# An index projection cut into blocks of 256 and 328 columns, its loads and gating transposes in another order, weight splits without one of their waits, and the first expert picks computed earlier

## The chip, the cores and the metric

One core of a Trainium2 chip runs the whole program. The metric is the device time of one execution in microseconds. The core has TensorE (PE in the profile; PEld is its loading of stationary operands), VectorE (DVE), ScalarE (ACT), GpSimd (POOL) and SyncE (SP), whose only work here is to issue DMAs. Line numbers such as L936 are those of the kernel before; behind the change they shift by one to some ten lines.

## What is computed

The program computes three transformer layers over 256 tokens of width 1024, in float32. The parts that the change touches are the input projection of the first layer, its expert layer, and the weights' preparation everywhere:

```python
q, k, v, qi, ki, wi, su, sv, ga, gb = split_columns(rms_norm(h, g) @ w_in)   # widths 1024 x3, 512, 64, 8, 1024 x4
qi, ki = rope(qi), rope(ki)                       # 8 index heads of 64, one key of 64
rel = relu(einsum('bqhd,bsd->bqhs', qi, ki)); score = einsum('bqh,bqhs->bqs', wi, rel)
sel = top_k(causal(score), 64)                    # then attention of q over the chosen keys, values
mixed = einsum('gts,bcsgd->bctgd', tril(sgu_w), layer_norm(gelu(sv))) + b_s   # gating weights sgu_w
g_sel = argmax(x @ w_group); e_in_group = (x @ w_er)[g_sel]; top2 -> experts, softmax -> gates
ys = (silu(x @ w_in[e])[:256] * ...) @ w_out[e]; out += gates * ys            # 32 experts, 2 per token
```

Behind the first layer come two more: attention and cross attention with a feed-forward of 2816, then a gated linear recurrence with cross attention and the same feed-forward.

## The kernel before

**Products in three parts.** Every weight matrix is used as a high and a low part. A linear block is up to 512 output columns wide and up to 8 row chunks (k) of 128 deep per piece. `linear` issues, for each k and each of two token tiles, three matmuls: high x high (L936), low weight x high input (L937), high weight x low input (L938); so a block of 8 k is 48 matmuls. `linear_turned` does the same with the weights stationary and 256 tokens moving (L966, L968, L969).

**The supply of weights.** SyncE loads piece n (L668) into one of two ring buffers as soon as the low parts of piece n-2 are made (`raw_free`). A piece is cut into units of two k. ScalarE copies a unit to `w_high` (L1529), which needs one of 8 unit slots to be free of the matmuls on the unit 8 before it; GpSimd then subtracts it to `w_low` (L863), and only then may TensorE use the unit. Each engine runs its program in order: where ScalarE splits pieces is written out by hand between its other jobs (`split_to`, `split_units`), and so it is on GpSimd.

**The index stage.** The blocks come in the order q0, q1, qi (512 columns: the 8 index heads), kw (72 columns: index key and head weights), k0, k1. Amid k = 4 and 5 of qi, TensorE transposes the gating weights sgu_w (L984; taken by ScalarE L1629 and VectorE L2106). Amid k0, at k = 6, it transposes the late row parameters (`later_columns`), the four pairs of rotated index heads and the index key. Between kw's load and k0's load SyncE issues 19 small loads (router weights, row parameters, gains; L679 to L713).

**The router and the experts.** After the first layer's output, VectorE works out the choice of experts (L2261 to L2305): the selection, then the gates' weights (L2293 to L2298), then each token's place in its expert's list (L2301), then the number of rounds (L2302 to L2305, `router_done`). TensorE meanwhile counts with small matmuls (L1204) and runs 34 and 14 filler matmuls (`keep_running`, L1196). Then come 8 batches of 4 experts: VectorE writes `picks` (L2317) and `gates` (L2319), TensorE gathers tokens (L1214), multiplies with the first weights (L1230), with the second (L1247) and adds back (L1256). Before the first batch TensorE waits for `router_done` and reads the number of rounds into a register. Expert weights (12 MB per batch) stream in as buffers come free.

**Norms behind a projection.** After the blocks o0, fo0 (layer one of the two later ones; `post_norm`), and o1, fo1 (`post_norm_by_rows`), ScalarE squares the result and takes a root. These projections have 12 or 22 row chunks, so two or three pieces per block. In these two functions ScalarE waits, before it splits the piece after n, until TensorE has used all of piece n-1 (`pieces_used(act, n - 1)`), beside the wait that each unit has for its own slot.

Of the kernel before, what the change touches and what calls it, by code (L numbers as in the profile page):

```python
# [120 lines left out]
def program(nc, io, upto=99, tap=None):  # L121
# [115 lines left out]
    with ctx:  # L237
# [209 lines left out]
        qi_roped = tok(buf(9, 1024, 1024))  # L447
        qi_T = feat(buf(8, 1024))
        ki_twice = tok(buf(8, 256, 1168))
# [212 lines left out]
        def _(sp):  # L662
# [36 lines left out]
            for n in range(RAW, router_piece):  # L699
                if n == RAW + 2:  # L700
# [129 lines left out]
        def _(pool):  # L830
# [37 lines left out]
            split_to(2)  # L868
# [45 lines left out]
        def _(pe):  # L914
# [85 lines left out]
            def both(x):  # L1000

                return lambda i: [(P * t, x[:, t, P * i:P * (i + 1)]) for t in range(TILES)]
# [94 lines left out]
            linear("k0", *from_x, ready=amid(6, later_columns, lambda: pe.wait_ge(roped, 2), lambda: turn("qi", 4, both(qi_roped)),  # L1097
                                             lambda: turn("ki", 1, both(ki_twice))))
# [111 lines left out]
            def expert_batch(it, nth, parity, firsts, extra=False):  # L1210
# [11 lines left out]
                pe.wait_ge(moe_x, 2 * it + 2)  # L1222
                for a in range(2):
# [245 lines left out]
        def _(act):  # L1469
# [269 lines left out]
            def post_norm_by_rows(i, name):  # L1739
# [3 lines left out]
                for j in range(2):  # L1743
                    _, used, _ = blocks[f"{name}{j}"]
                    for n, _, _ in used[1:]:
                        if j == 1 and n == used[-1][0]:
                            split_to(n)
                        else:
                            pieces_used(act, n - 1)
                            split_to(n + 1)  # L1750
# [22 lines left out]
            def post_norm(i, name, late_split=False):  # L1773

                nth = (i - 5) // 2
                for j in range(2):
                    _, used, _ = blocks[f"{name}{j}"]
                    late = late_split and j == 1
                    for n, _, _ in used[1:]:
                        pieces_used(act, n - 1)  # L1780
# [203 lines left out]
        def _(dve):  # L1984
# [121 lines left out]
            tr_take(dve, 1, "sgu_w", 4, lambda i, ps: dve.tensor_copy(sgu_wT[:, SEQ * i:SEQ * (i + 1)], ps))  # L2106
# [555 lines left out]
```

## Time and profile before

| | us |
|---|---|
| median of three runs (lowest, highest) | 1335.0 (1333.69, 1336.3) |
| the profiled execution, whole | 1331.26 |
| its span in the trace | 1329.5 |
| TensorE busy within the span | 1244.0 |
| GpSimd, ScalarE, VectorE busy | 770.9, 637.9, 463.8 |
| granted TensorE clock, mean | 0.994 |

The profiled execution was 1.76 us longer than its span, and 3.7 us shorter than the median. A granted clock of 1.00 is 2.4 GHz and 0.50 is 1.2 GHz. TensorE's busy time counts pipelined matmuls by modelled ends, so how fast it really goes is read from the distance of one start to the next.

### The profile page before, as it was taken

The page shows a single profiled execution, that of the slowest core. Times are in us where ns is not written, and L with a number is a line of the kernel's source. Part 1 is how long each engine was busy: PE and PEld are TensorE (multiplying, and loading weights), DVE is VectorE, ACT ScalarE, POOL GpSimd, SP SyncE. Part 2 cuts the span into 40 slices and gives each one's busy share as a digit, 9 for nine tenths or more (in the row PEclk, how much of TensorE's full clock was granted, in tenths as well). Part 3 has the DMA queues.
Part 4 walks back from the last instruction along what each step waited for, and adds up shares of the span by engine and source line. Part 5 has one row for each costly group of instructions (what it writes and reads, how often), then busy time and mean ns, then how long its engine had stood idle before and what let it go on. Part 6 is the DMA issues. An engine that isn't in the chain of part 4 may idle for free.

```text
span 1329.5 us, 19674 instructions
## 1 busy us (share of the span) xinstructions
PE 1244.0 (94%) x7904; PEld 1022.0 (77%) x7904; DVE 463.8 (35%) x1047; ACT 637.9 (48%) x1108; POOL 770.9 (58%) x345
## 2 busy tenths in 40 slices
PE   8999999998888887999899999999999889999998
PEld 6888877776343333888789999889997778999986
DVE  3527343433121112356513333113468272322211
ACT  6345544653111011746646555446797444644452
POOL 6868985440000000981168988888689805788884
PEclk9899999999999999999999999999999999999999
DMA  7635554298999999452035655544444503455552
GB/s 252 213 128 190 190 189 158 102 364 340 422 421 377 422 422 412 179 189 80 33 127 170 211 191 183 198 174 155 163 143 174 199 8 127 157 177 176 189 190 79
DMA packets 127041, 275.09 MB, mean 207 GB/s; under 512 B 7604, under 2 KB 53996, under 8 KB 115180
## 3 DMA queue, kind: packets, MB, share of 16 engines
q1 hardware_dynamic: 126668, 272.86, 56.2%
q8 instruction: 58, 0.95, 0.3%
q10 hardware_dynamic: 288, 1.05, 0.2%
q14 instruction: 27, 0.22, 0.1%
HBM read 272.85 MB, written 1.05 MB: 206 GB/s over the span
## 4 chain that ended last, share of the span: by engine, by line
PE 73%; DMA 8%; ACT 7%; DVE 5%; POOL 4%; issue 2%; SPq 0%; POOLq 0%; DVEq 0%; ACTq 0%
PE lin_ps L936 11%; PE lin_ps L938 11%; PE lin_ps L937 11%; PE lin_ps L966 8%; PE lin_ps L969 8%; PE lin_ps L968 8%; POOL w_low L863 4%; DMA ring<-in_w_expert_in 4%; PE sc_ps L1230 3%; ACT w_high L1529 2%; DMA work<-in_w_expert_out 2%; PE lin_ps L1247 2%; PE lin_ps L1052 2%; PE sc_ps L1021 2%; PE lin_ps L1214 1%
## 5 line engine op out<-in xcount | busy, mean ns | idle before, releaser
L863 POOL TENSOR_TENSOR w_low<-ring,w_high 128x1024 fp32r<-128x1024 f32 (+1 forms) x318 | 761.5, 2435 | 467.0 <-ACT w_high L1529 466.9
L1529 ACT ACTIVATE w_high<-ring 128x1024 fp32r<-128x1024 f32 (+1 forms) x320 | 312.5, 1042 | 136.4 <-PE lin_ps L938 78.6
L966 PE MATMUL lin_ps<-x_high,w_high 128*128 128x256 f32 x960 | 272.8, 284 | 0.0
L968 PE MATMUL lin_ps<-x_high,w_low 128*128 128x256 f32 x960 | 271.6, 283 | 0.0
L969 PE MATMUL lin_ps<-x_low,w_high 128*128 128x256 f32 x736 | 208.3, 283 | 0.0
L966 PEld LDWEIGHTS lin_ps<-x_high,w_high 128*128 128x128 f32 x960 | 184.2, 192 | 0.3 <-DVEq L2442 0.2
L968 PEld LDWEIGHTS lin_ps<-x_high,w_low 128*128 128x128 f32 x960 | 184.3, 192 | 0.1
L936 PE MATMUL lin_ps<-w_high,x_high 128*128 128x512 f32 (+1 forms) x432 | 170.2, 394 | 5.2 <-POOL w_low L863 2.6
L937 PE MATMUL lin_ps<-w_low,x_high 128*128 128x512 f32 (+1 forms) x432 | 167.7, 388 | 0.0
L938 PE MATMUL lin_ps<-w_high,x_low 128*128 128x512 f32 (+1 forms) x368 | 142.8, 388 | 0.0
L969 PEld LDWEIGHTS lin_ps<-x_low,w_high 128*128 128x128 f32 x736 | 141.2, 192 | 0.0
L936 PEld LDWEIGHTS lin_ps<-w_high,x_high 128*128 128x128 f32 x432 | 82.0, 190 | 22.6 <-DVE w_low L2074 2.8
L937 PEld LDWEIGHTS lin_ps<-w_low,x_high 128*128 128x128 f32 x432 | 82.1, 190 | 15.8
L938 PEld LDWEIGHTS lin_ps<-w_high,x_low 128*128 128x128 f32 x368 | 70.0, 190 | 14.3
L1812 ACT ACTIVATE attn<-lin_ps,cols 128x256 f32<-128x256 f32 x44 | 18.5, 471 | 115.3 <-PE lin_ps L969 115.3
L936 PE MATMUL lin_ps<-w_high,hidden_high 128*128 128x512 f32 x176 | 68.7, 390 | 0.7 <-POOL w_low L863 0.7
L1230 PE MATMUL sc_ps<-ring,work 128*32 128x512 f32 x480 | 57.3, 624 | 12.2 <-DMA ring<-in_w_expert_in 7.7
L937 PE MATMUL lin_ps<-w_low,hidden_high 128*128 128x512 f32 x176 | 68.5, 389 | 0.0
L938 PE MATMUL lin_ps<-w_high,hidden_low 128*128 128x512 f32 x176 | 68.5, 389 | 0.0
L2428 DVE SCALAR_TENSOR_TENSOR attn<-lin_ps,cols,attn 128x255 f32<-128x255 f32 x44 | 21.1, 478 | 125.4 <-ACT attn L1812 125.4
L969 PE MATMUL lin_ps<-u_low,w_high 128*128 128x256 f32 x224 | 63.4, 283 | 0.0
L1230 PEld LDWEIGHTS sc_ps<-ring,work 128*32 128x32 f32 x480 | 15.3, 114 | 49.3 <-issue 36.8
(434 smaller groups left out, 1914.3 us busy)
## 6 DMA issues: line engine op xcount, KB each, us to landing
ring<-in_w_expert_in SPq DMA_DIRECT2D x30, 2048.0 KB, 15.7
ring<-in_ffn_w_in SPq DMA_DIRECT2D x44, 1024.0 KB, 7.7
ring<-in_w_in SPq DMA_DIRECT2D x13, 2048.0 KB, 7.9
ring<-in_b_w_in SPq DMA_DIRECT2D x11, 2048.0 KB, 8.0
work<-in_w_expert_out SPq DMA_DIRECT2D x8, 2048.0 KB, 23.0
ring<-in_w_expert_out SPq DMA_DIRECT2D x8, 2048.0 KB, 22.6
ring<-in_ffn_w_out SPq DMA_DIRECT2D x8, 2048.0 KB, 7.9
ring<-in_a_w_in SPq DMA_DIRECT2D x4, 2048.0 KB, 8.1
```

The lines of the kernel that those rows point to most:

```text
L863: pool.tensor_tensor(w_low[:, slot, 0:words], raw, w_high[:, slot, 0:words].bitcast(F32), ALU.subtract).then_inc(low_made, 1)
L936: pe.matmul(out[:, t, :], high(k)[:, at], wh[:, j, :], start=(k == 0), stop=False)
L937: pe.matmul(out[:, t, :], high(k)[:, at], wl[:, j, :], start=False, stop=False)
L938: mm = pe.matmul(out[:, t, :], low(k)[:, at], wh[:, j, :], start=False, stop=(k == last_k))
L966: pe.matmul(out, wh[:, j, at], high(k), start=(k == 0 and f < 2), stop=False, skip_group_check=True)
L968: pe.matmul(out, wl[:, j, at], high(k), start=False, stop=False, skip_group_check=True)
L969: mm = pe.matmul(out, wh[:, j, at], low(k), start=False, stop=(k == last_k), skip_group_check=True)
L1021: mm = pe.matmul(sc_ps[:, g % 2, SEQ * t:SEQ * t + n], q(i, t), k(i)[:, 0:n], start=True, stop=True)
L1052: mm = pe.matmul(out[:, dim * t:dim * (t + 1)], pT[:, P * n:P * (n + 1)], v(i, c), start=(c == 0), stop=(c == chunks[-1][0]))
L1230: mm = pe.matmul(hid_ps[CAP * e:CAP * (e + 1), :], gathered[:, 4 * a + k, CAP * e:CAP * (e + 1)], extra_slot(e)[k // 2][:, k % 2, :] if ex ...
L1247: mm = pe.matmul(y_ps[CAP * e:CAP * (e + 1), n, :], act_T[:, P * f + CAP * e:P * f + CAP * (e + 1)], w, start=(f == 0), stop=(f == 1))
L1529: act.activation(w_high[:, slot, 0:words], raw, ACT.Copy).then_inc(high_made, 1)
```

## The change

The index projection's 584 columns are no longer cut into 512 + 72 but into 256 (four heads) + 328 (four heads, key, head weights). The transposes of sgu_w move from qi to kw. The 19 small loads are issued behind k0's load, not ahead of it. ScalarE and GpSimd take the gating weights later. The rotated heads lie in two buffers. In the post norms the wait for whole pieces is gone. In the first expert batch VectorE makes places and picks first, then the gates, and the round count between its two gathers; TensorE's wait for the count comes ahead of the batch's first expert matmul, and its register load after the whole batch.

```diff
-            weight_block("qi", [(w_in, starts["qi"], 512)], 512)
-            weight_block("kw", [(w_in, starts["kw"], 72)], 72)
+            weight_block("qi", [(w_in, starts["qi"], 256)], 256)
+            weight_block("kw", [(w_in, starts["qi"] + 256, 328)], 328)
...
             for n in range(RAW, router_piece):
-                if n == RAW + 2:
+                if n == RAW + 3:
                     load_router()
...
-            split_to(2)
+            split_to(blocks["k0"][1][0][0])
             tr_wait(pool, "sgu_w", 4)
...
-            linear("qi", *from_x, ready=sgu_weights)
-            linear("kw", *from_x)
+            linear("qi", *from_x)
+            linear("kw", *from_x, ready=sgu_weights)
...
+                pe.wait_ge(router_done, 1)
                 for a in range(2):
...
-            pe.wait_ge(router_done, 1)
+            expert_batch(0, 0, 0, 32)
             n_rounds = pe.value_load(rounds[0:1, 0:1], min_val=1, max_val=SEQ // CAP)
-            expert_batch(0, 0, 0, 32)
             expert_batch(1, 0, 1, None, extra=True)
...
             copy_scaled("q1", half(q_raw, 1))
+            lin_ready(act, "qi")
+            split_to(piece("qi") + 2)
             tr_take(act, 0, "sgu_w", 4, lambda i, ps: act.activation(sgu_wT[:, SEQ * i:SEQ * (i + 1)], ps, ACT.Copy))
-            for name in ("qi", "kw"):
-                lin_ready(act, name)
-                split_to(piece(name) + 2)
+            lin_ready(act, "kw")
+            split_units(sum(units[piece("kw") + 2]) - 2)
             tr_take(act, 0, "qi", 4, plain(qi_T))
+            split_to(piece("kw") + 2)
...
                     for n, _, _ in used[1:]:
-                        pieces_used(act, n - 1)
                         split_to(n if late else n + 1)
...
+                dve.tensor_tensor(pick4, place, slots_iota, ALU.is_equal).then_inc(moe_pick, 1)
+                if opening:
+                    make_gates()
+                dve.wait_ge(moe_pick, it + 1)
+                dve.tensor_tensor(gate4, pick4, weight, ALU.mult).then_inc(moe_gate, 1)
...
+                    if opening and a == 0:
+                        count_rounds()
```

On ScalarE, from the sines of the rotation to the copy of k0 (L1551/L1552), the program of before and then that of the change read as follows; L1529/L1530 is the making of high parts, `xqT` the gating weights, `work<-tr_ps` the transposed index heads:

```order
L1627 ACTIVATE attn<-sc_ps 128x192
L1551 ACTIVATE work<-lin_ps,small 128x512 x2
L1529 ACTIVATE w_high<-ring 128x144 x4
L1629 ACTIVATE xqT<-tr_ps 128x256 x2
L1529 ACTIVATE w_high<-ring 128x1024 x8
L1567 ACTIVATE work<-tr_ps 128x256 x2
L1551 ACTIVATE work<-lin_ps,small 128x512 x2
L1529 ACTIVATE w_high<-ring 128x1024 x4
```

```order
L1628 ACTIVATE attn<-sc_ps 128x192
L1552 ACTIVATE work<-lin_ps,small 128x512 x2
L1530 ACTIVATE w_high<-ring 128x656 x4
L1530 ACTIVATE w_high<-ring 128x1024 x4
L1632 ACTIVATE xqT<-tr_ps 128x256 x2
L1530 ACTIVATE w_high<-ring 128x1024 x2
L1568 ACTIVATE work<-tr_ps 128x256 x2
L1530 ACTIVATE w_high<-ring 128x1024 x2
L1552 ACTIVATE work<-lin_ps,small 128x512 x2
```

The four units of kw grow from 144 to 656 words; k0's units now stand ahead of the gating weights, and two of k1's units ahead of the transposed heads.

On GpSimd, from its first constants to the mask of the scores (L876), before and after; L870 is the mask of the gating weights:

```order
L851 MEMSET eps 128x1
L863 TENSOR_TENSOR w_low<-ring,w_high 128x1024 x10
L870 AFFINE_SELECT xqT<-xqT 128x1024
L863 TENSOR_TENSOR w_low<-ring,w_high 128x144 x4
L863 TENSOR_TENSOR w_low<-ring,w_high 128x1024 x16
L876 AFFINE_SELECT attn<-attn 128x512
```

```order
L851 MEMSET eps 128x1
L863 TENSOR_TENSOR w_low<-ring,w_high 128x1024 x6
L863 TENSOR_TENSOR w_low<-ring,w_high 128x512 x4
L863 TENSOR_TENSOR w_low<-ring,w_high 128x656 x4
L863 TENSOR_TENSOR w_low<-ring,w_high 128x1024 x4
L870 AFFINE_SELECT xqT<-xqT 128x1024
L863 TENSOR_TENSOR w_low<-ring,w_high 128x1024 x12
L876 AFFINE_SELECT attn<-attn 128x512
```

The ten full units ahead of the mask become six full, four of 512 words (qi), four of 656 (kw) and four full ones (k0).

On VectorE, in the router, before and after; L2296 to L2298 (L2300 to L2302) weight the gates, L2301 (L2291) adds the places, L2302 to L2305 (L2306 to L2309) count the rounds, L2317 (L2318) writes the picks:

```order
L2295 TENSOR_TENSOR small<-small 128x2
L2296 TENSOR_TENSOR work<-work,small 128x2x32
L2297 TENSOR_TENSOR work<-work,small 128x2x32
L2298 TENSOR_TENSOR work<-work 128x2x32
L2301 TENSOR_TENSOR work<-work,sc_ps 128x2x32
L2302 TENSOR_REDUCE small<-sc_ps 128x1
L2303 TENSOR_SCALAR work<-iota,small 128x8
L2304 TENSOR_REDUCE small<-work 128x1
L2305 CAST rounds<-small 128x1
L2309 UNCONDITIONAL_BRANCH
L2309 ISA
L2317 TENSOR_TENSOR work<-work,iota 128x256
```

```order
L2291 TENSOR_TENSOR work<-work,sc_ps 128x2x32
L2318 TENSOR_TENSOR work<-work,iota 128x256
L2297 SCALAR_TENSOR_TENSOR small<-small 128x2
L2298 RECIPROCAL small<-small 128x2
L2299 TENSOR_TENSOR small<-small 128x2
L2300 TENSOR_TENSOR work<-work,small 128x2x32
L2301 TENSOR_TENSOR work<-work,small 128x2x32
L2302 TENSOR_TENSOR work<-work 128x2x32
L2322 TENSOR_TENSOR work<-work 128x256
L2326 TENSOR_TENSOR work<-lin_ps,moe_gain 128x512
L2306 TENSOR_REDUCE small<-sc_ps 128x1
L2307 TENSOR_SCALAR work<-iota,small 128x8
```

The places and the picks now come first, and the round count behind the first gather (L2326). The first two batches are written out, and the loop starts at the third.

## Rows read from the trace of the kernel before

**Rows 1.** The page: busy time of each engine, and the shares of the ending chain

```profile
PE 1244.0 (94%) x7904; PEld 1022.0 (77%) x7904; DVE 463.8 (35%) x1047; ACT 637.9 (48%) x1108; POOL 770.9 (58%) x345
...
PE 73%; DMA 8%; ACT 7%; DVE 5%; POOL 4%; issue 2%; SPq 0%; POOLq 0%; DVEq 0%; ACTq 0%
```

**Rows 2.** Windows, from:to, length; busy PE, PEld, DVE, ACT, POOL (instructions); clock; DMA; GB/s

```profile
46.40:51.80 5.40, 5.40 (x49) 5.40 (x47) 4.86 (x12) 3.90 (x4) 3.56 (x2) 0.96 0.91 304
...
51.80:56.00 4.20, 4.16 (x11) 3.28 (x11) 3.33 (x18) 0.87 (x1) 4.20 (x3) 0.50 0.32 117
...
286.00:293.00 7.00, 4.72 (x26) 3.25 (x26) 4.51 (x10) 3.22 (x8) 0.00 (x0) 1.00 0.79 296
...
326.00:328.00 2.00, 2.00 (x24) 0.52 (x16) 0.00 (x0) 0.00 (x0) 0.00 (x0) 1.00 0.00 0
...
740.00:820.00 80.00, 80.00 (x669) 80.00 (x668) 23.99 (x56) 41.87 (x70) 67.05 (x30) 1.00 0.60 197
```

**Rows 3.** Timeline of TensorE, index stage: start us, us, engine line

```profile
34.54 0.39 PE L936 MATMUL lin_ps<-w_high,x_high 128*128 128x512 f32 x1
...
34.76 0.39 PE L937 MATMUL lin_ps<-w_low,x_high 128*128 128x512 f32 x1
...
46.36 0.20 PE L936 MATMUL lin_ps<-w_high,x_high 128*128 128x72 f32 x1
...
52.16 0.80 PE L936 MATMUL lin_ps<-w_high,x_high 128*128 128x512 f32 x1
...
63.28 0.66 PE L984 MATMUL tr_ps<-ident,work 104*128 104x104 f32 x5
```

**Rows 4.** Timeline of TensorE, second feed-forward

```profile
1149.89 0.28 PE L966 MATMUL lin_ps<-x_high,w_high 128*128 128x256 f32 x1
...
1150.01 0.28 PE L968 MATMUL lin_ps<-x_high,w_low 128*128 128x256 f32 x1
```

**Rows 5.** Timeline of ScalarE, index stage

```profile
39.31 0.97 ACT L1529 ACTIVATE w_high<-ring 128x144 fp32r<-128x144 f32 x4
...
47.10 3.90 ACT L1529 ACTIVATE w_high<-ring 128x1024 fp32r<-128x1024 f32 x4 [4.27 <-DMA ring<-in_w_in]
...
55.13 3.90 ACT L1529 ACTIVATE w_high<-ring 128x1024 fp32r<-128x1024 f32 x4 [4.13 <-DMA ring<-in_w_in]
```

**Rows 6.** Timeline of GpSimd, index stage

```profile
16.85 11.84 POOL L863 TENSOR_TENSOR w_low<-ring,w_high 128x1024 fp32r<-128x1024 f32 x5 [1.26 <-ACT w_high L1529]
...
43.97 1.87 POOL L863 TENSOR_TENSOR w_low<-ring,w_high 128x144 fp32r<-128x144 f32 x4
...
48.24 18.72 POOL L863 TENSOR_TENSOR w_low<-ring,w_high 128x1024 fp32r<-128x1024 f32 x8 [2.40 <-ACT w_high L1529]
```

**Rows 7.** Timeline of SyncE's queue, index stage

```profile
29.13 0.58 SPq L679 DMA_DIRECT2D router_w<-in_w_router_group  x1
...
39.08 18.91 SPq L668 DMA_DIRECT2D ring<-in_w_in  x3
```

**Rows 8.** Timeline of TensorE, router and first expert batches

```profile
316.67 1.92 PE L1196 MATMUL lin_ps<-mem_high 128*128 128x256 f32 x14
...
319.94 3.83 PE L1214 MATMUL lin_ps<-work 128*128 128x128 f32 x32 [1.35 <-DVE work L2317]
```

**Rows 9.** Timeline of VectorE, router

```profile
317.83 0.22 DVE L2301 TENSOR_TENSOR work<-work,sc_ps 128x64 f32<-128x64 f32 x1
...
319.01 0.43 DVE L2317 TENSOR_TENSOR work<-work,iota 128x256 f32<-128x256 f32 x1
```

**Rows 10.** Timeline of TensorE: its waits for split weights around o0, o1, fo1

```profile
694.47 0.36 PE L966 MATMUL lin_ps<-mem_high,w_high 128*128 128x256 f32 x1 [0.55 <-POOL w_low L863]
...
1119.44 0.50 PE L936 MATMUL lin_ps<-w_high,cross_high 128*128 128x512 f32 x1 [0.45 <-POOL w_low L863]
...
1316.62 0.50 PE L936 MATMUL lin_ps<-w_high,hidden_high 128*128 128x512 f32 x1 [0.68 <-POOL w_low L863]
```

**Rows 11.** Timeline of ScalarE at o0

```profile
672.20 5.80 ACT L1529 ACTIVATE w_high<-ring 128x1024 fp32r<-128x1024 f32 x6 [10.52 <-PE lin_ps L938]
```

More of the change, by code:

```diff
@@ L998, in made, with both @@
                 return lambda k: parts_made(pe, name, k + 1)
-            def both(x):
-                return lambda i: [(P * t, x[:, t, P * i:P * (i + 1)]) for t in range(TILES)]
+            def both(x, before=0):
+                return lambda i: [(P * t, x[:, t, P * (i - before):P * (i - before + 1)]) for t in range(TILES)]
             def small_out(pe, name):
@@ L1095, in later_columns @@
                 turn("later_cols", 1, lambda i: [(0, rows[0:104, 0, :]), (104, rows[0:120, 1, :]), (224, rows[0:88, 2, :])])
[L1097 to L1098 removed]
+            linear("k0", *from_x, ready=amid(6, later_columns, lambda: pe.wait_ge(roped, 2), lambda: turn("qi", 2, both(qi_roped)),
+                                             lambda: turn("qi", 4, both(qk_roped, 2), first=2),
+                                             lambda: turn("ki", 1, both(qk_roped, -2))))
             linear("k1", *from_x)
@@ new lines, in count_rounds, with expert_batch @@
+            def count_rounds():
+                step(dve.tensor_reduce(small[:, 26:27], counts[:, 2, :], AX, ALU.max))
+                step(dve.tensor_scalar(spare[:, 0, 0:8], iota[:, 2, 0:8], small[:, 26:27], None, ALU.is_lt))
+                step(dve.tensor_reduce(small[:, 27:28], spare[:, 0, 0:8], AX, ALU.add))
+                dve.tensor_copy(rounds[:], small[:, 27:28]).then_inc(router_done, 1)
+            slots_iota = iota[:, 0:1, :].unsqueeze(1).broadcast_to([P, TILES, BATCH, CAP])
+            def expert_batch(b, it, opening=False):
+                place = places[:, :, b].unsqueeze(3).broadcast_to([P, TILES, BATCH, CAP])
+                weight = gate[:, :, b].unsqueeze(3).broadcast_to([P, TILES, BATCH, CAP])
+                pick4 = picks.rearrange("p t (e s) -> p t e s", e=BATCH)
+                gate4 = gates.rearrange("p t (e s) -> p t e s", e=BATCH)
+                dve.tensor_tensor(pick4, place, slots_iota, ALU.is_equal).then_inc(moe_pick, 1)
[3 more added lines that the diff above has]
+                dve.tensor_tensor(gate4, pick4, weight, ALU.mult).then_inc(moe_gate, 1)
+                for a in range(2):
+                    dve.wait_ge(moe_gathered, 2 * it + a + 1)
+                    gains = moe_gain[:, 4 * a:4 * a + 4].unsqueeze(2).broadcast_to([P, 4, P])
+                    dve.tensor_tensor(gathered[:, 4 * a:4 * a + 4, :], gather_ps[:, 4 * a:4 * a + 4, :], gains, ALU.mult)\
+                        .then_inc(moe_x, 1)
+                    if opening and a == 0:
+                        count_rounds()
+                dve.wait_ge(moe_silu, it + 1)
+                dve.tensor_tensor(act_out, silu_out, hid_ps[:, D_EXPERT:2 * D_EXPERT], ALU.mult).then_inc(moe_act, 1)
+                for n in range(2):
+                    dve.wait_ge(moe_back, 2 * it + n + 1)
+                    for t in range(TILES):
+                        ins = dve.tensor_tensor(h[:, t, NB * n:NB * (n + 1)], back_ps[n][:, t, :],
+                                                h[:, t, NB * n:NB * (n + 1)], ALU.add)
+                    ins.then_inc(moe_added, 1)
@@ L2310, in expert_round @@
+            def expert_round(r, first=0):
+                with dve.Fori(first, BATCHES // 2) as pair:
                     for parity in range(2):
                         b = 2 * pair + parity
-                        it = r * BATCHES + b
-                        place = places[:, :, bass.ds(b * BATCH, BATCH)].unsqueeze(3).broadcast_to([P, TILES, BATCH, CAP])
-                        weight = gate[:, :, bass.ds(b * BATCH, BATCH)].unsqueeze(3).broadcast_to([P, TILES, BATCH, CAP])
-                        pick4 = picks.rearrange("p t (e s) -> p t e s", e=BATCH)
```

67 lines of the change are left out of this document (22 added, 45 removed).

## The prediction

> **What bounds the kernel now.** I began with the page: TensorE is busy 94% of the span, GpSimd 58%, and the chain that ended last runs 73% through TensorE, with 8% DMA and 4% GpSimd [rows 1]. So an edit gains what it takes off TensorE's stream or its waits. The windows then show where TensorE is slow without being idle: from 46.4 to 51.8 (kw) it is busy all the time at clock 0.96, from 51.8 to 56 still busy but at 0.50, that is 1.2 GHz [rows 2]. The timeline gives the marks of that stage: qi starts at 34.54, kw at 46.36, k0 at 52.16, and k0's first six chunks, 36 matmuls, last until the transposes at 63.28 [rows 3]; the pace of 256-wide matmuls stands in a later stage [rows 4]. The third view is the supply: ScalarE, GpSimd and SyncE in the same stage [rows 5 to 7]. The fourth is the router [rows 8, 9], the fifth TensorE's waits for split weights late in the program [rows 10, 11].
>
> **The index blocks.** TensorE's pace first. Two 256-wide matmuls in a feed-forward start 0.12 apart [rows 4]; 256 columns at 2.4 GHz are 0.107, which leaves 0.0133 fixed. For 512 columns that gives 0.2267 (the row shows 0.22 [rows 3]), for 328 columns 0.150. Old: qi 11.82, of which 48 x 0.2267 = 10.88 is matmuls and 0.94 the gating transposes; kw 52.16 - 46.36 = 5.80, 0.121 for each narrow matmul, as much as 256 columns cost. New: qi 48 x 0.12 = 5.76, kw 48 x 0.150 = 7.20, and the 0.94 of transposes, now in kw. That is 13.90 instead of 17.62.
>
> The rule of the Trainium skill speaks against this saving: "TensorE: Matmul & The Clock Gate", Back-to-back issue gap, gives N / 2.4 + 2.5 ns per matmul with a floor near 25 ns, by which 48 matmuls of 512 and 48 of 72 columns cost 11.9 us (estimate) and 48 of 256 and 48 of 328 cost 11.9 too. The row has 0.121 per narrow matmul, four times that floor, so the row decides and the saving stands.
>
> Is the supply fast enough? kw's high parts are made behind the copy of q1, which waits for the sines, from 39.31 [rows 5]. A unit of 1024 words costs ScalarE 3.90 / 4 = 0.98, one of 144 words 0.97 / 4 = 0.24; 656 words lie at 0.67. GpSimd takes 11.84 / 5 = 2.37 and 1.87 / 4 = 0.47 [rows 6], so 1.57 for 656 and 1.26 for 512. The first kw unit is ready at 39.31 + 0.67 + 0.1 + 1.57, about 41.7. TensorE is through with the new qi at 34.54 + 5.76 = 40.3, so **a new wait of 1.4** stands ahead of kw. After it TensorE needs 1.8 per unit against 1.57, no wait. k0 would start at 41.7 + 7.20 + 0.94 = 49.8 instead of 52.16: **2.3**.
>
> k0's own weights: q1's low parts end at 16.85 + 11.84 = 28.69 [rows 6], qi's at 28.69 + 4 x 1.26 = 33.7, so its load is issued then, not at 39.08 behind the small loads [rows 7]; it landed 8.0 after its issue (47.10 [rows 5]), so now near 41.7. ScalarE is free for it at 42, done at 45.9, in time for the gating transposes. GpSimd ends kw at 46.4 and k0's first unit at 48.8, one microsecond before its use. The small loads occupy SyncE for 39.08 - 29.13 = 9.95, now 34.1 to 44.1. k1's load waits for kw's low parts until 46.4; it took 9.3 (from GpSimd's end at 45.84 to 55.13), so it lands near 55.7, and ScalarE, which now stands on it with two units ahead of the index transposes, is free at 57.6. TensorE asks at 49.8 + 36 x 0.2267 = 58.0. Cover 0.4, and if it is gone, the stall goes one to one into the end. VectorE's rotation of five heads instead of one costs some 2 us more but ends near 54.5, ahead of the same 58.0. GpSimd's mask of the gating weights is not needed for 100 us.
>
> **The clock.** Old k0: 63.28 - 52.16 = 11.12 for 36 matmuls, at full speed 8.16. If the narrow matmuls are what preceded the fall and 80 us of 256-wide ones run at 1.00 [rows 2], the new stage keeps its clock: **2.96** more. TensorE is idle 1.4 in it; between 286 and 293 it was idle 2.3 at clock 1.00 [rows 2]. Bounds of the whole part: 2.3 if the clock falls all the same, 6.7 if the wait of 1.4 does not come; I take 5.3. The v, su and sv blocks, attention and the expert loads all start by TensorE's progress, so they move with it.
>
> **The first picks.** TensorE's first gather waited 1.35, until 319.94, for picks written at 319.01; 14 fillers run from 316.67 for 1.92 before it [rows 8, 9]. The six gate steps and four count steps leave the path. TensorE's counts are issued by 316.67, so the places (0.22, now from about 316.9) and the picks (0.43) end near 317.6, so the fillers, which end at 318.6, are the limit: **1.35**, all of the wait and no more. The gates (six steps of some 0.23) end near 319.4, ahead of the first half of the gather, and the count lies behind that half, while TensorE gathers the other; TensorE's register load now lies in its wait ahead of the second batch. Will the expert stream swallow this? At 326 to 328 the DMA engines are idle (0.00) [rows 2], waiting for the first batch to free its buffer. So the stream behind it starts earlier by the full amount. Bounds 0 and 1.35.
>
> **The post norms.** At o0 ScalarE stood 10.52 until 672.20 for a piece that it could have split unit by unit [rows 11], and GpSimd, at 2.37 per unit, came late for TensorE. The waits in which this ends are 0.55, 0.45 and 0.68 [rows 10]; at fo0 TensorE has none. Without the piece waits the splits, and the loads behind the low parts, run about 8 us earlier, more than any of these: **1.7**. Bounds 0 and 2.2 (a little more if ScalarE's square at o1 comes sooner). Nothing is added, so I exclude a loss.
>
> **Sum.** 5.3 + 1.35 + 1.7 = 8.3. The profiled execution of 1331.26 becomes 1322.9; the median was 3.7 above it, so 1335.0 - 8.3 = **1326.7**.
>
> **Rivals.**
> 1. *The clock falls in the index stage all the same.* For it: TensorE was not idle when it fell, and the new stage has a gap of 1.4. Against: the two windows at 1.00. It costs the 2.96: 1329.7.
> 2. *ScalarE's new order stalls TensorE.* Its cover is 0.4 at k0's index transposes, and nearly nothing at the gating transposes, where ScalarE must be through with k0's four units. k0 or k1 landing 1 to 5 later gives a stall of about 3: 1329.7.
> 3. *The widths save nothing*, which is what the skill's rule above says. By rows, as a mechanism: the cost would lie in the columns alone. The 2.3 is lost: 1329.0. The 0.121 per narrow matmul is against it.
> 4. *The expert stream takes the gains of the front.* If the loads between 290 and 324 end where they did, the first two parts are lost and the third stays: 1333.3. For it: the DMA engines are at 0.8 and more in most of that time (0.79 from 286 to 293 [rows 2]). Against: every one of these loads waits for a ring buffer or a product that moves too, and the idle window at 326.
> 5. *Slower: the small loads get in front of k1.* They now stand in SyncE's queue between k0 and k1. At 9.95 they leave it free 2.3 before k1's load is due. The cover at the index transposes is 0.4, so to lose 8.3 + 2.7 k1 must slip by 11.4, and the small loads must last 13.7 longer, 23.7 in all, because their packets queue behind k0's 2 MB. From there on the change is slower: 1337.7. Nothing in the rows shows such an issue time.
>
> **How the numbers follow.** Forecast 0.58, rival one 0.12, two 0.13, three 0.03, four 0.08, five 0.06. The forecast's own range is 1324.0 to 1328.5. For 8 in 10 I go from 1323.0 (no wait before kw, all bounds up, the runs' own spread of 1.3) to 1331.2 (rivals one to three with that spread). A difference under 0.2%, 2.7 us, is not told from none. Faster: forecast and rivals one to three, 0.86; the same: rival four, 0.08; slower: 0.06.
>
> **What would show it.** In the changed trace: 256-wide matmuls 0.12 and 328-wide ones 0.15 apart; a wait of 1.4 for GpSimd ahead of kw; clock 1.00 from 46 to 60; k1's first matmul 5.3 earlier than before. First gather with no wait for VectorE, the gather another 1.35 earlier in relation to the router's counts, and the stream's end earlier by 6.6. No wait for `w_low` at o0, o1 and fo1. What would make it wrong: clock 0.50 anywhere in the stage, a wait of TensorE at the gating or index transposes, or an end of the expert stage that did not move.

## The result, and the profile after

The changed kernel takes 1327.6 us (median of four runs, 1325.92 to 1327.97) against 1335.26 before (four runs). The ratio is 0.9941, with a 95% interval of 0.9924 to 0.9958: 7.7 us faster, 10.1 to 5.6. The forecast was 1326.7, with a range of its own from 1324.0 to 1328.5. Two later timings of the same kernel gave ratios of 0.9946 (0.9928 to 0.9964) and 0.9940 (0.9920 to 0.9961). Three of the 74 executions of the kernel before in the experiments took 1391.82 to 2079.93 at a mean granted clock of 0.88 to 0.55, and no number here counts them.

The profiled execution of the changed kernel took 1327.43, span 1325.7. That is only 3.8 below the span before, half of what the medians say, so the first task is to see why. From the page of the changed kernel, busy time and the chain that ended last:

```profile
PE 1243.0 (94%) x7904; PEld 1023.8 (77%) x7904; DVE 456.4 (34%) x1044; ACT 638.2 (48%) x1108; POOL 771.0 (58%) x345
...
PE 76%; ACT 7%; DMA 7%; DVE 5%; POOL 2%; issue 2%; SPq 0%; DVEq 0%; ACTq 0%; POOLq 0%
```

TensorE is as busy as before; GpSimd's share of the chain fell from 4% to 2%. Windows of the same trace (columns as in [rows 2]), first the opening, then the index stage:

```profile
12.00:16.00 4.00, 3.78 (x10) 3.04 (x11) 2.08 (x4) 1.53 (x3) 2.29 (x1) 0.59 1.05 376
...
46.00:52.00 6.00, 5.44 (x37) 4.96 (x35) 1.79 (x7) 2.51 (x4) 6.00 (x4) 1.00 0.42 123
52.00:56.00 4.00, 4.00 (x20) 3.29 (x19) 3.51 (x11) 0.00 (x0) 4.00 (x3) 1.00 0.88 270
56.00:62.00 6.00, 4.62 (x25) 3.52 (x24) 2.45 (x4) 2.27 (x3) 2.36 (x2) 1.00 1.02 375
62.00:68.00 6.00, 5.74 (x21) 4.47 (x21) 1.27 (x3) 2.72 (x4) 6.00 (x4) 0.72 0.38 147
```

The reader is to see three things. From 12 to 16 the granted clock was 0.59, in code that the change doesn't touch; the kernel before had 1.00 there, and this execution starts qi 1.9 late for it. From 46 to 56 the clock is 1.00, where [rows 2] had 0.96 and then 0.50. And from 56 to 62 TensorE works only 4.62 of 6.00, with a clock of 0.72 behind it; the kernel before idled 0.72 at its index transposes. The timeline of TensorE shows that gap (columns as in [rows 3], with the idle time before an instruction in brackets):

```profile
36.48 0.28 PE L936 MATMUL lin_ps<-w_high,x_high 128*128 128x256 f32 x1
36.59 0.28 PE L937 MATMUL lin_ps<-w_low,x_high 128*128 128x256 f32 x1
...
42.23 0.32 PE L936 MATMUL lin_ps<-w_high,x_high 128*128 128x328 f32 x1
42.39 0.31 PE L937 MATMUL lin_ps<-w_low,x_high 128*128 128x328 f32 x1
...
48.18 0.44 PE L984 MATMUL tr_ps<-ident,work 128*128 128x128 f32 x2 [0.56 <-ACT xqT L1632]
...
51.16 0.39 PE L936 MATMUL lin_ps<-w_high,x_high 128*128 128x512 f32 x1
...
59.35 0.66 PE L984 MATMUL tr_ps<-ident,work 104*128 104x104 f32 x5
...
61.82 0.66 PE L984 MATMUL tr_ps<-ident,work 128*128 128x128 f32 x4 [0.95 <-ACT work L1568]
62.74 0.44 PE L984 MATMUL tr_ps<-ident,work 128*128 128x128 f32 x2 [0.26 <-ACT work L1568]
62.93 0.63 PE L936 MATMUL lin_ps<-w_high,x_high 128*128 128x512 f32 x1
```

qi takes 5.75 and no wait stands ahead of kw; k0 starts 14.68 after qi, before 17.62 [rows 3]. But the index transposes, 2.45 long before (from 63.28 [rows 3] to k1's first matmul at 65.73), now take 3.58 (59.35 to 62.93), because ScalarE takes them late. Before, TensorE waited there only for VectorE:

```profile
64.36 0.66 PE L984 MATMUL tr_ps<-ident,work 128*128 128x128 f32 x4 [0.42 <-DVE cols L2134]
65.32 0.66 PE L984 MATMUL tr_ps<-ident,work 128*128 128x128 f32 x4 [0.30 <-DVE work L1994]
65.73 0.47 PE L936 MATMUL lin_ps<-w_high,x_high 128*128 128x512 f32 x1
```
Why ScalarE is late stands in its own timeline:

```profile
59.50 2.00 ACT L1530 ACTIVATE w_high<-ring 128x1024 fp32r<-128x1024 f32 x2 [10.46 <-DMA ring<-in_w_in]
```

And in SyncE's queue, start and length of issues:

```profile
36.72 3.20 SPq L679 DMA_DIRECT2D router_w<-in_w_router_expert  x1
39.96 3.26 SPq L704 DMA_DIRECT2D work<-in_norm_g  x1
...
50.54 29.30 SPq L668 DMA_DIRECT2D ring<-in_w_in  x4
```

The small loads hold SyncE from 36.09 to 50.54, 14.45 instead of the 9.95 of [rows 7]; two of them take 3.20 and 3.26, where the kernel before had 0.92 and 0.82. The second ends at 43.22, just before k0's 2 MB landed (43.85 in the trace). k1's load goes out at 50.54, ScalarE begins on it at 59.50, and it has stood on it for 10.46 while TensorE's transposes wait.

**Leads.** The lead of a trace is how much earlier than in the kernel before it reaches the same place. To see where time comes from along a whole execution, I took the same instruction of VectorE in two traces and subtracted its starts (before minus the other). The first column is the start in the trace of before, the values are the lead in us.

| at | index part alone | picks alone | post norms alone | changed | changed, third time | rest behind k1 |
|---|---|---|---|---|---|---|
| 29 | 0.23 | -2.35 | 0.24 | -1.95 | 0.06 | 0.30 |
| 102 | 2.80 | -0.83 | 0.36 | 1.19 | 5.34 | 6.51 |
| 306 | 2.90 | -2.33 | 0.36 | 1.27 | 3.78 | 6.53 |
| 332 | 1.79 | -0.72 | 0.36 | 2.41 | 5.40 | 6.15 |
| 650 | 1.63 | -1.14 | 0.24 | 2.33 | 5.31 | 5.91 |
| 745 | 1.64 | -1.18 | 1.17 | 3.29 | 6.23 | 6.87 |
| 1091 | 1.60 | -1.23 | 1.11 | 3.28 | 6.21 | 6.85 |
| 1134 | 0.05 | -2.81 | 0.58 | 2.71 | 7.28 | 7.89 |
| 1319 | 0.05 | -2.81 | 1.69 | 3.82 | 8.39 | 9.00 |

A drop of 1.1 to 1.6 (by 306, 332 or 1134), and of 2 to 3 at 29, is a spell of half clock that one execution has there and another has not; such spells come at a few places and are different in each execution. Without them the steps are plain: the stage up to 102, the picks between 306 and 332, the post norms ahead of 745, 1134 and 1319.

### The profile page after: what moved, and what is told of

It is laid out like the page before. It is cut to its first block, busy times and chain, and to the rows that moved or that the text cites. A ratio compares the mean times of both kernels' runs of the same rounds, so it can differ in the third digit from the quotient of the medians.

```text
span 1325.7 us, 19664 instructions
## 1 busy us (share of the span) xinstructions
PE 1243.0 (94%) x7904; PEld 1023.8 (77%) x7904; DVE 456.4 (34%) x1044; ACT 638.2 (48%) x1108; POOL 771.0 (58%) x345
## 4 chain that ended last, share of the span: by engine, by line
PE 76%; ACT 7%; DMA 7%; DVE 5%; POOL 2%; issue 2%; SPq 0%; DVEq 0%; ACTq 0%; POOLq 0%
PE lin_ps L936 11%; PE lin_ps L937 11%; PE lin_ps L938 11%; PE lin_ps L966 8%; PE lin_ps L968 8%; PE lin_ps L969 8%; DMA ring<-in_w_expert_in 4%; PE sc_ps L1232 4%; DMA work<-in_w_expert_out 2%; POOL w_low L863 2%; ACT w_high L1530 2%; PE lin_ps L1249 2%; PE lin_ps L1052 2%; PE sc_ps L1021 2%; PE lin_ps L1215 1%
## 5 line engine op out<-in xcount | busy, mean ns | idle before, releaser
L1530 ACT ACTIVATE w_high<-ring 128x1024 fp32r<-128x1024 f32 (+1 forms) x320 | 313.7, 1043 | 109.1 <-DMA ring<-in_ffn_w_out 34.5
L936 PE MATMUL lin_ps<-w_high,x_high 128*128 128x512 f32 (+2 forms) x432 | 168.9, 391 | 5.1 <-POOL w_low L863 2.6
L937 PE MATMUL lin_ps<-w_low,x_high 128*128 128x512 f32 (+2 forms) x432 | 166.5, 385 | 0.0
L938 PE MATMUL lin_ps<-w_high,x_low 128*128 128x512 f32 (+2 forms) x368 | 141.5, 385 | 0.0
L1232 PE MATMUL sc_ps<-ring,work 128*32 128x512 f32 x480 | 57.3, 626 | 12.1 <-DMA ring<-in_w_expert_in 7.7
```

The lines of the kernel that those rows point to most:

```text
L936: pe.matmul(out[:, t, :], high(k)[:, at], wh[:, j, :], start=(k == 0), stop=False)
L937: pe.matmul(out[:, t, :], high(k)[:, at], wl[:, j, :], start=False, stop=False)
L938: mm = pe.matmul(out[:, t, :], low(k)[:, at], wh[:, j, :], start=False, stop=(k == last_k))
L1232: mm = pe.matmul(hid_ps[CAP * e:CAP * (e + 1), :], gathered[:, 4 * a + k, CAP * e:CAP * (e + 1)], extra_slot(e)[k // 2][:, k % 2, :] if ex ...
L1530: act.activation(w_high[:, slot, 0:words], raw, ACT.Copy).then_inc(high_made, 1)
```

## The experiments

All ran beside the kernel before, and ratios are to it. There are twelve kernels in three groups of four; each group has its own executions of the kernel before.

**The parts alone.** Each takes the hunks of the change that belong to it and leaves the rest as before; `whole_again` is the changed kernel.

```diff
 only_index:  weight_block 256 + 328, rope and transposes to match, n == RAW + 3, order of turns
 only_picks:  expert_batch(0, ...) ahead of make_gates() and count_rounds(), router_done per batch
 only_post:
-                            pieces_used(act, n - 1)
                             split_to(n + 1)
```

(The first two are described in words; of the third the main line is shown.)

> The kernel before with the index part alone: widths 256 and 328, the new turns, the order of the loads and of ScalarE. Theory (the parts add up and this one is the 5.3 of the prediction, less what the late landing of k1 took): 4.5 to 5.5 us faster than before. Rival (the late k1, the waits of 0.95 and 0.26 at the index transposes and the half clock behind them, about 3.5 us, are a loss of every execution, and the index part is worth only its widths): 2 to 3 us faster. The trace should have a wait of TensorE for ScalarE near 62 us and clock 0.50 behind it in both.

> The kernel before with the first picks alone ahead of the gates and the count. Theory: the first gather loses its wait of 1.35 and the expert stream moves by as much, so 1.2 to 1.4 us faster. Rival (the expert stream takes it back): within 0.3 of before, with the first gather earlier and the last expert batch where it was.

> The kernel before without ScalarE's waits for used pieces in the post norms. Theory: the waits of 0.55, 0.45 and 0.68 at o0, o1 and fo1 go, 1.7 us faster. Rival (the loads that now run earlier meet others, or other waits take their place): 0 to 1 us faster, with a wait for w_low or for a piece left at one of the three.

> The changed kernel once more, beside its three parts. Theory (the parts add up): 7.7 us faster than before, the sum of the three parts within 1 us. In the profiled execution before it TensorE ran at 0.59 of its clock from 12 to 16 us, where the kernel before ran at 1.00: if that is chance of an execution, this trace may show 1.00 there and a span 2 us shorter, about 1324; if it came with the change, it is 0.59 again.

| kernel | median us | ratio (95%) | that is, us |
|---|---|---|---|
| only_index | 1331.66 | 0.9978 (0.9965 to 0.9990) | -2.9 |
| only_picks | 1334.05 | 0.9995 (0.9982 to 1.0008) | -0.7 |
| only_post | 1331.93 | 0.9978 (0.9964 to 0.9991) | -2.9 |
| whole_again | 1327.72 | 0.9946 (0.9928 to 0.9964) | -7.2 |

The last column is (ratio - 1) times 1335. The parts sum to 6.5 against 7.2, which is additive within the intervals. The index part is worth 2.9, about half of its 5.3 (interval 1.3 to 4.7): its rival holds. The post norms are worth more than 1.7. For the picks the interval includes nothing and 1.35; the leads decide there. They grow by 1.61 and 1.62 in two traces (-2.33 to -0.72, 3.78 to 5.40). Both had lost 1.6 to a spell of half clock shortly before, but it does not come back by itself: `kw_padded`, which has the same spell and not the picks, has a lead of -1.60 at 306 and -1.59 at 332. Of the gain, 0.1 (third time) and 0.4 (picks alone) are gone by 650, so the expert stream takes little or nothing back. The question on the opening is answered as chance: of the 14 traces 8 had a spell of half clock between 10 and 18, `whole_again` (span 1325.1) and `only_picks` among them, and 6 had none, the kernel before and `whole_third` among them.

In `only_index` the opening ran at full clock, so it compares directly with the kernel before (its TensorE):

```profile
57.16 0.66 PE L984 MATMUL tr_ps<-ident,work 104*128 104x104 f32 x5
...
60.24 0.66 PE L984 MATMUL tr_ps<-ident,work 128*128 128x128 f32 x4 [1.57 <-ACT work L1568]
...
61.50 0.78 PE L936 MATMUL lin_ps<-w_high,x_high 128*128 128x512 f32 x1
```

Against [rows 3] the transposes start 6.1 sooner (57.16 for 63.28), k1 4.2 sooner (61.50 for 65.73), and the scores behind k1, after another spell of half clock, 2.8 sooner (76.64 for 79.46).

**Is it k1's landing?** `rest_behind_k1` moves loads in SyncE's queue, `turns_first` takes ScalarE off k1's load, `both_edits` does both, and `kw_padded` asks the kernel before about the clock.

```diff
 rest_behind_k1:
                 if n == RAW + 3:
-                    load_router()
                     for matrix, at, cnt, view in row_loads():
...
+                if n == RAW + 4:
+                    load_router()
                     sp.dma_start(gain[:], io["sgu_norm_g"][0].partition_broadcast(P)).then_inc(gain_in, 16)
 turns_first:
             lin_ready(act, "kw")
-            split_units(sum(units[piece("kw") + 2]) - 2)
             tr_take(act, 0, "qi", 4, plain(qi_T))
 kw_padded (on the kernel before):
-            weight_block("kw", [(w_in, starts["kw"], 72)], 72)
+            weight_block("kw", [(w_in, starts["kw"], 256)], 256)
```

> The changed kernel, with the router's weights and the small loads that the index stage doesn't need moved behind k1's load in SyncE's queue; only the rows for the column transposes stay ahead of it. Theory (k1 lands late because SyncE is held by small loads until about 50, while kw's low parts free its buffer near 44 to 46): k1's load is issued some 4 us earlier, lands by 55, the waits of 0.95 to 1.57 and 0.26 at the index transposes go, and the run is 1.5 to 2 us faster than the changed kernel, which is 9 to 10 faster than before; 3 more if the half clock behind the transposes came from that stall. Rival (the loads moved behind delay v0's weights): no gain, with a wait of TensorE for w_low at v0.

> The changed kernel, with ScalarE taking the index transposes before it splits k1's first two units. Theory (the stall at the transposes is ScalarE standing on k1's load, nothing else): the waits of 1.2 to 1.8 us for it go; k1's first low part is ready about 63.5 against TensorE's need at 62.3 (both as in an execution whose opening ran at full clock), so a new wait of 0.5 to 1 appears ahead of k1: 0.5 to 1.5 us faster than the changed kernel. Rival (GpSimd's chain of k1's units, 2.4 each, sets k1's pace): no gain or up to 1 slower.

> Both edits on the changed kernel: the loads behind k1, and the index transposes ahead of k1's units on ScalarE. Theory: with k1 landed by 55 ScalarE splits it after the transposes from about 59 on, later than in the kernel that has the loads moved alone, so a wait of about 1 for k1's low parts comes in: 1 us slower than that one, and about as fast as turns_first. Rival: as fast as rest_behind_k1.

> The kernel before, with kw's block 256 columns wide instead of 72 (184 of them unused columns of the next weight); a matmul of 256 columns costs 0.120 like one of 72 with 0.121. Theory of the prediction (the narrow matmuls precede the fall of the clock): clock 1.00 from 46 to 60, up to 3 us faster than before, less what the wider load costs. Rival (the half clock comes in every execution somewhere in the first 70 us, whatever the widths; the executions so far have it at 12 to 16, at 52 to 56 or at 61 to 66): half clock again in one of these places, and not faster than before; 0 to 2 slower from the wider splits.

| kernel | median us | ratio (95%) |
|---|---|---|
| rest_behind_k1 | 1324.45 | 0.9926 (0.9906 to 0.9946) |
| turns_first | 1328.45 | 0.9956 (0.9941 to 0.9971) |
| both_edits | 1326.68 | 0.9939 (0.9918 to 0.9961) |
| kw_padded | 1333.03 | 0.9991 (0.9979 to 1.0004) |

SyncE's queue in `rest_behind_k1`:

```profile
44.30 0.39 SPq L668 DMA_DIRECT2D ring<-in_w_in  x1
...
45.36 3.67 SPq L679 DMA_DIRECT2D router_w<-in_w_router_expert  x1
49.08 4.37 SPq L707 DMA_DIRECT2D gain<-in_sgu_norm_g  x1
```

ScalarE there:

```profile
53.80 2.01 ACT L1531 ACTIVATE w_high<-ring 128x1024 fp32r<-128x1024 f32 x2 [7.38 <-DMA ring<-in_w_in]
57.45 0.38 ACT L1569 ACTIVATE work<-tr_ps 128x256 f32<-128x256 f32 x1 [1.64 <-PE tr_ps L985]
```

TensorE there, at the last index transposes and the first matmul behind them:

```profile
58.80 0.66 PE L985 MATMUL tr_ps<-ident,work 128*128 128x128 f32 x4 [0.30 <-DVE work L1993]
59.21 0.47 PE L937 MATMUL lin_ps<-w_high,x_high 128*128 128x512 f32 x1
```

k1's load goes out at 44.30, lands at 53.8, and now ScalarE waits for TensorE (1.64) and no longer the reverse; k1 starts at 59.21 instead of 61.50 in `only_index`. The theory holds, and v0, the next block, shows no wait. The router's expert load and the one behind it still take 3.67 and 4.37, now where nobody waits for them. The ratio gives 9.9 us, 2 to 3 more than the changed kernel, but the intervals overlap.

`turns_first` did what it should at the transposes (no wait for ScalarE there; 0.3 for k1's low parts instead) and lost it elsewhere. It was not faster than the changed kernel, as its rival said. VectorE at the head scores:

```profile
75.92 3.45 DVE L2142 TENSOR_SCALAR attn<-attn,wi 128x256 f32<-128x256 f32 x2 [15.01 <-ACT attn L1642]
```

GpSimd ahead of and beside it:

```profile
60.38 18.84 POOL L863 TENSOR_TENSOR w_low<-ring,w_high 128x1024 fp32r<-128x1024 f32 x8 [5.60 <-ACT w_high L1530]
```

TensorE, the second half of the scores:

```profile
80.11 5.46 PE L1106 MATMUL sc_ps<-work 128*128 128x256 f32 x16 [2.18 <-ACT attn L1642]
```

GpSimd's run of k1's and v0's units ends at 79.22; VectorE's first two score steps, 0.62 in the trace of `only_index`, where GpSimd had ended at 77.85, last 3.45 here and end at 79.4. TensorE waits 2.18 for them, and the clock falls behind that. Neither theory had this cause. `both_edits` lies 2.2 us above `rest_behind_k1` (1326.68 against 1324.45), more than its theory's 1, though the intervals overlap; its TensorE has the wait for k1's low parts (0.29) and again 2.21 at the scores.

`kw_padded` speaks for the theory of the clock. Its window, from 52 to 56:

```profile
52.00:56.00 4.00, 3.25 (x24) 2.95 (x23) 3.32 (x12) 3.33 (x4) 3.44 (x2) 1.00 0.94 307
```

The window of `only_post`, whose index stage is that of before:

```profile
51.80:56.00 4.20, 4.20 (x12) 3.33 (x12) 3.25 (x18) 1.01 (x2) 4.20 (x3) 0.50 0.25 95
```

A single trace could be luck, so I also took (1 - clock) times the span, the time that half clock stands for, over all runs: 11.3 us (standard error 0.4, 71 runs) for the kernel before, 8.2 (0.3, 12 runs) for `kw_padded`. It wins about 3.0 by the clock, gives back 0.75 in a new wait for the wider low parts ahead of k0 and about 1 more that I have not traced, and ends 1.2 below before, within its interval of no change.

**The repaired order beside the changed kernel, and what the order is worth alone.** `rest_again` is `rest_behind_k1` once more, `whole_third` the changed kernel, `index_rest` is `only_index` and `before_rest` the kernel before, both with the same edit of the loads as above.

> The changed kernel with the loads that the stage doesn't need behind k1's load, once more and beside the changed kernel. Theory (1.8 of waits gone, and the half clock of the first 90 us comes less often since TensorE neither runs 72-wide matmuls nor stands at the transposes): 2 to 4 us faster than the changed kernel of the same call, 9.5 to 11 faster than before. Rival (the first result was luck of six runs): within 1 of the changed kernel.

> The changed kernel again. Both theories: 7 to 8 us faster than before. In the trace a wait of 1.2 to 1.9 for ScalarE at the index transposes.

> The index part alone on the kernel before, with the loads that the stage doesn't need behind k1's. Theory (the prediction's 5.3 was right for a k1 that lands in time): 5 to 6 us faster than before, 2 to 3 more than the index part gave alone. Rival (the index part is worth its widths, 3, whatever k1 does): 3 to 4.

> The kernel before, with only that: the rows ahead of k0 as before, the other small loads behind k1's. Theory (the gain of that order comes from a late k1, and the kernel before has none): no difference, within 1 us, with half clock from 52 to 56 behind the 72-wide matmuls. Rival (fewer small loads in the stage help whatever the widths, by the clock or the queue): 2 to 3 us faster.

| kernel | median us | ratio (95%) |
|---|---|---|
| rest_again | 1325.28 | 0.9935 (0.9911 to 0.9959) |
| whole_third | 1325.43 | 0.9940 (0.9920 to 0.9961) |
| index_rest | 1328.70 | 0.9962 (0.9950 to 0.9975) |
| before_rest | 1333.37 | 0.9998 (0.9983 to 1.0012) |

`index_rest` is 5.1 us faster than before, where `only_index` was 2.9: with k1 in time, the index part is worth about what the prediction put on it. The two ran in different groups and their intervals overlap; by mean spans, each against the kernel before beside it, the difference is 2.1 with a standard error of 0.8. `before_rest` is no faster, so the order of loads has no worth of its own. `rest_again` is within 1 us of the changed kernel beside it, as its rival said. Over all its runs the mean span is 1322.7 (standard error 0.6, 12 runs), and 1324.9 (0.4, 16 runs) for the changed kernel. That difference of 2.2 compares across groups: counted from the kernel before beside each it is 1.6 (0.8), and side by side in the last group 0.4. A gain is probable, and not settled. The trace of `whole_third` says why they can meet, and it misses its expectation of a wait of 1.2 to 1.9. ScalarE at k1's first units:

```profile
56.74 2.00 ACT L1530 ACTIVATE w_high<-ring 128x1024 fp32r<-128x1024 f32 x2 [9.73 <-DMA ring<-in_w_in]
```

Its windows:

```profile
56.00:62.00 6.00, 5.16 (x28) 3.77 (x27) 2.17 (x5) 4.55 (x6) 4.12 (x2) 1.00 0.89 327
62.00:68.00 6.00, 6.00 (x28) 4.95 (x27) 0.00 (x0) 4.77 (x6) 6.00 (x4) 1.00 0.00 0
```

Here k1 landed at 56.74, the waits at the transposes were 0.23 and 0.19, and the clock stayed at 1.00. The stage in all traces: the columns up to the landing are counted from qi's first matmul, the last one from the start of the span. The head scores are the products of index heads and key; k1's landing is the start of ScalarE's first unit of it behind a wait for the load, and where it did not wait, the place is empty.

| kernel | k0 | index transposes | k1 | head scores | k1 landed | half clock, 46 to 68 |
|---|---|---|---|---|---|---|
| before | 17.62 | 28.74 | 31.19 | 44.92 | 20.6 | 51.3 to 58.2 |
| only_post | 17.62 | 28.62 | 31.07 | 44.80 | 20.7 | 50.9 to 57.7 |
| only_picks | 17.62 | 27.20 | 29.64 | 43.37 | 20.6 | 53.9 to 57.3 |
| before_rest | 17.63 | 28.68 | 31.13 | 44.85 | 20.8 | 53.5 to 60.3 |
| kw_padded | 18.49 | 26.74 | 29.18 | 42.90 | 23.1 | none |
| only_index | 14.66 | 22.85 | 27.19 | 42.33 | 23.6 | 61.1 to 64.5 |
| after | 14.68 | 22.87 | 26.45 | 41.76 | 23.0 | 63.1 to 66.5 |
| whole_again | 14.65 | 22.87 | 26.84 | 40.58 | 23.4 | none |
| whole_third | 14.63 | 22.84 | 25.70 | 39.43 | 22.3 | none |
| turns_first | 14.70 | 22.91 | 25.36 | 39.65 | | none (81.5 to 85.0) |
| both_edits | 14.44 | 22.65 | 25.10 | 39.37 | | none |
| rest_behind_k1 | 14.31 | 22.53 | 24.98 | 38.69 | 19.6 | none |
| rest_again | 14.08 | 22.29 | 24.74 | 38.47 | 19.6 | none |
| index_rest | 14.15 | 22.35 | 24.80 | 38.52 | 19.5 | none |

## Why the prediction was right

The time was, within 1 us. The sum owes part of that to luck: of the three terms one was too large in most executions and two too small, and these errors offset. Two of the signs that were to make the prediction wrong came in the profiled execution, a wait of TensorE for ScalarE at the gating and at the index transposes and half clock inside the stage.

**Widths: right, and more.** 0.12 and 0.15 apart, as worked out (qi's 48 take 5.75; kw's start at 42.23, 42.39 and 42.54). The rule of the Trainium skill named in the prediction would have saved nothing in these 96 matmuls; qi and kw took 17.62 before and 14.65 after. The same section of the Trainium skill says of its rule that it counts too little at small N in a stream with weight loads, and the 0.111 below, for 72 columns, agrees. One reading was off: the 0.121 per 72-wide matmul is an average that holds the start of the half clock. These rows of the kernel before show both paces:

```profile
49.40 0.28 PE L937 MATMUL lin_ps<-w_low,x_high 128*128 128x72 f32 x1
49.51 0.28 PE L938 MATMUL lin_ps<-w_high,x_low 128*128 128x72 f32 x1
...
51.30 0.40 PE L936 MATMUL lin_ps<-w_high,x_high 128*128 128x72 f32 x1
51.50 0.41 PE L937 MATMUL lin_ps<-w_low,x_high 128*128 128x72 f32 x1
```

At full clock they stand 0.111 apart, so 0.4 to 0.5 of the 3.7 put on the widths (17.62 less 13.90) belonged to the clock; the sum of the two is the same.

The **new wait of 1.4** ahead of kw did not come: it rested on kw's high parts at 39.31, which I took over from before. They started at 37.16 in `only_index`. What let them start was VectorE, which computes the angles that ScalarE's sines wait for. This step in the trace of before:

```profile
32.07 2.34 DVE L2087 TENSOR_SCALAR work<-work,pos_f 128x96 f32<-128x96 f32 x1
```

The same step in `only_index`:

```profile
31.84 0.44 DVE L2090 TENSOR_SCALAR work<-work,pos_f 128x96 f32<-128x96 f32 x1
```

This is no chance of one execution: the step takes 2.12 to 2.34 in all five traces with the old qi block and 0.43 to 0.44 in all nine with the narrower one, where GpSimd's units on qi beside it are 512 words and no longer 1024. Instead there was 0.53 to 0.56 at the gating transposes. In all, k0 started 3.0 sooner in the stage, not 2.3.

**The supply of k1: wrong.** "The small loads occupy SyncE for 39.08 - 29.13 = 9.95, now 34.1 to 44.1" is the step that failed. They took 13.9 to 15.7 in the four traces of the changed stage, k1 landed 22.3 to 23.6 after qi's start and not 21.2, and TensorE asks at 22.85. So rival two came in all four, with waits for ScalarE of 0.4 to 1.8 instead of 3, and its cause was the one that I had looked at under rival five. I had written that nothing in the rows shows such an issue time, and that was true; I had moved the loads behind one of 2 MB and kept a price read behind one of 0.29 MB. The traces hold a better way to price them. In all 14 the issue behind the router's expert weights ends 0.25 to 1.0 before the weight load ahead of the two has landed, in the kernel before at 31.53 for kw's landing at 32.22: until then SyncE is held. The other 17 issues took 7.0 there, until 38.57 (not 39.08, when k0's load followed). With k0's landing forecast near 41.7, that puts k1's issue at about 48 (an estimate from these rows) and its landing, 9.3 later, at about 57.3 instead of 55.7; in `only_index`, whose stage began at 34.31, it was 49.57 and 57.92.

**The clock: right in kind.** With 72-wide matmuls the clock fell between 50.9 and 53.9 in four traces of four, in each while the last of them ran; with 256 and more it fell there in none of ten. But in two of the four traces of the changed stage it fell at 61.1 and 63.1 instead, right behind the stall, and in none of the four with the loads moved. That widths hold the clock in this stretch is shown; that the stall brought it down is likely, with `whole_again` (1.34 of wait, no fall) against it. Together the stage gained 3.2, 2.6, 4.3 and 5.5 in the four traces, 3.9 on average, and 6.2 to 6.5 with k1 in time; forecast 5.3.

Not all of that gain lasts. Between 286 and 314 of the span all ten traces with blocks of 256 and more have a spell of half clock, and of the four with 72 columns only `only_picks` has one. `whole_third`, then the kernel before:

```profile
286.00:291.00 5.00, 4.71 (x15) 3.72 (x16) 0.23 (x1) 0.00 (x0) 0.00 (x0) 0.66 1.01 423
```

```profile
280.00:320.00 40.00, 33.76 (x202) 28.35 (x200) 17.59 (x62) 18.22 (x40) 0.00 (x0) 1.00 0.95 380
```

Over all runs half clock stands for 9.4 us (standard error 0.6, 16 runs) in the changed kernel and 11.3 (0.4) in the kernel before: 1.9 less, where the prediction had 2.96. What brings the later spell is not tested.

**The picks: right, slightly small.** 1.6 for 1.35. TensorE in `whole_third`, the fillers and the first gather:

```profile
312.88 1.91 PE L1197 MATMUL lin_ps<-mem_high 128*128 128x256 f32 x14
314.63 3.74 PE L1215 MATMUL lin_ps<-work 128*128 128x128 f32 x32
```

The picks on VectorE there:

```profile
313.41 0.42 DVE L2318 TENSOR_TENSOR work<-work,iota 128x256 f32<-128x256 f32 x1
```

The fillers are the limit, as forecast: 1.75 from their start to the gather, against 3.27 in [rows 8], that is 1.52; the gather itself is 0.09 shorter. Rival four is out: most of the lead from here is still there at 650.

**The post norms: right in kind, mis-sized.** All three waits of [rows 10] are gone, but the leads grow by 0.92, 1.07 and 1.11, 3.1 in all and not 1.7; timed alone, 2.9. I had priced the stalls by their idle time. The rows of the kernel before on both sides of the middle one:

```profile
1118.61 0.39 PE L938 MATMUL lin_ps<-w_high,cross_low 128*128 128x512 f32 x1
...
1119.78 0.39 PE L937 MATMUL lin_ps<-w_low,cross_high 128*128 128x512 f32 x1
```

The stalled matmul started at 1119.44 [rows 10]. From start to start that is 0.83 and then 0.34, where these matmuls stand 0.227 apart, so it cost 0.60 + 0.11 = 0.71; the idle time says 0.45, since it counts from a modelled end 0.39 behind the start. In the same way the one at o0 comes to 0.79 and that at fo1 to 0.94. These make 2.4 of the 3.1. The rest lies at three places of TensorE's stream: between the kernel before and `whole_third` the lead grows by 0.16 at 732.20, by 0.11 at 1314.62, and by 0.35 at 1132.90, at transposes that wait for the norm behind o1:

```profile
1132.90 0.66 PE L994 MATMUL tr_ps<-ident,work 128*128 128x128 f32 x4 [1.08 <-DVEq L2416]
```

In `whole_third`:

```profile
1125.62 0.66 PE L994 MATMUL tr_ps<-ident,work 128*128 128x128 f32 x4 [0.76 <-DVEq L2429]
```

Before, ScalarE stood on a load in the middle of that norm, and with the change it does not (the prediction had this in its bounds, as a little more at o1):

```profile
1123.01 1.06 ACT L1529 ACTIVATE w_high<-ring 128x1024 fp32r<-128x1024 f32 x1 [0.80 <-DMA ring<-in_ffn_w_in]
```

**Why the sum held:** 3.9 + 1.6 + 3.1 = 8.6 by the traces, 7.2 to 8.0 by the timings, 8.3 forecast. The first term was 1.4 too large and the other two 1.7 too small together. The traces' sum leaves out the later spell of half clock, which costs up to 1.6; that it explains the difference from the timings is likely, and not shown.

## What to carry to other kernels

Price a stall by the distance between the starts of neighbours, not by the idle time in brackets. When a queue's instructions are moved, their issue times don't move with them: look at what is in flight ahead of them in the new place and when it will land, and keep loads that are slow to issue and that nobody needs soon out of any gap in which a large one is due. Compare two traces by the lead of the same instruction at many places; spells of half clock show there as drops at one place, which the difference of two spans leaves mixed with the rest. Then ask whether the spells of one kernel come more often at a new place, which needs many executions.

## What the hardware showed that I had not expected

- A small load can hold SyncE's queue for long: the router's expert weights take 0.8 to 0.9 behind kw's 0.29 MB, 1.11 behind the 1 MB of `kw_padded`, and 3.1 to 3.7 behind a 2 MB block, and the load next in line goes from 0.8 to 1.0 up to 2.58, to 3.0 to 3.4 behind k0's block, and to 4.3 to 4.5 behind k1's. The ones after those take 0.3 to 0.7 in all cases, apart from a single one now and then. In all 14 traces the second of the two ends 0.25 to 1.0 before the weight load ahead has landed; the order without the expert weights behind k0 shows none above 0.7 there.
- An elementwise step of VectorE can last as long as GpSimd is inside a unit: 2.34 for 0.44 at the angles, 3.45 for 0.62 at the scores. The Trainium skill, "SBUF — State Buffer", Who interferes with whom, has the two engines share a port pair that one of them locks for a whole instruction. The trace agrees in that the long step at the scores ended 0.15 behind GpSimd's run; the port as such was not tested here.
- Half clock is granted in spells at a handful of places, in some executions and not in others. A short one costs 1.6 where TensorE is the bound, and the longer one of the kernel before cost 2.96 in k0 alone. Executions of the kernel before had a mean clock from 0.986 to 0.994 and spans from 1337.9 to 1328.9 to go with it. That is most of what differs between runs of one kernel here.
